# Thirteen more turns of activations by transposing DMA instead of TensorE

## The reference

```
def first_block(x, ...):
    proj = rmsnorm(x, norm1_w) @ w_in                    # feeds two branches, y_a and y_b
    mixed = gate_a * (y_a @ w_branch_a) + gate_b * (y_b @ w_branch_b)
    x = x + mixed @ w_out
    gu = rmsnorm(x, norm2_w) @ w_gate_up                 # 2048 -> 2 x 5632
    x = x + (silu(gu[:5632]) * gu[5632:]) @ w_down       # 5632 -> 2048
    return rmsnorm(x, norm_f_w)

def second_block(x, ...):
    proj = rms_norm(x, attn_norm_g) @ w_in               # feeds two token mixers
    h = x + concatenate([gla_out, nsa_out]) @ w_out
    m = rms_norm(h, ffn_norm_g)
    return h + (silu(m @ w_gate) * (m @ w_up)) @ w_down
```

## Time and profile before

| | us |
|---|---|
| median of 3 runs | 2662.98 |
| profiled execution, its own time | 2662.39 |
| its span, from first to last instruction | 2660.5 |
| TensorE busy in it | 2633.9 (99%) |
| ScalarE busy | 1329.6 (50%) |
| GpSimd busy | 1191.8 (45%) |
| VectorE busy | 1065.1 (40%) |

### The profile page before, as it was taken

How to read it: one execution, slowest core, us unless ns; L and a number is a source line. 1 busy time by engine, 2 the same in 40 slices (tenths; PEclk the granted TensorE clock), 3 DMA queues, 4 the chain that set the end, 5 groups by cost and what they waited for, 6 DMA issues and landing times. The chain is left out here.

```text
span 2660.5 us, 30430 instructions
## 1 busy us (share of the span) xinstructions
PE 2633.9 (99%) x12124; PEld 2172.7 (82%) x12124; DVE 1065.1 (40%) x1251; ACT 1329.6 (50%) x1654; POOL 1191.8 (45%) x535
## 2 busy tenths in 40 slices
PE   8999999999999999999999999999999999999999
PEld 6888787788888888888888878878888888888887
DVE  6577754433332222223332357446432322222222
ACT  6545445444445555555444465555455555554333
POOL 3576553344444444444444446333344444444443
PEclk9999999999999999999999999999999999999999
DMA  6444454365555666666555544454456666665554
GB/s 249 175 173 162 145 187 169 143 220 185 182 189 199 204 212 203 202 208 205 188 202 195 208 146 148 157 202 143 143 185 211 201 208 205 208 205 191 202 206 145
DMA packets 116844, 499.57 MB, mean 188 GB/s; under 512 B 50795, under 2 KB 53836, under 8 KB 59360
## 3 DMA queue, kind: packets, MB, share of 16 engines
q1 hardware_dynamic: 116704, 497.64, 54.5%
HBM read 485.02 MB, written 2.10 MB: 183 GB/s over the span
## 5 line engine op out<-in xcount | busy, mean ns | idle before, releaser
L2681 POOL TENSOR_TENSOR WL<-RAW,WH 128x1024 fp32r<-128x1024 f32 x441 | 1074.8, 2437 | 1423.0 <-ACT WH L1177 1422.8
L1177 ACT ACTIVATE WH<-RAW 128x1024 fp32r<-128x1024 f32 x889 | 939.6, 1058 | 1219.6 <-PE PB L633 1201.8
L1826 DVE TENSOR_TENSOR WL<-RAW,WH 128x1024 fp32r<-128x1024 f32 x448 | 603.8, 1348 | 1490.8 <-ACT WH L1177 1490.5
L629 PE MATMUL PB<-WH,HNH 128*128 128x512 f32 x2464 | 972.2, 395 | 5.1 <-ACT WH L1177 2.3
L633 PE MATMUL PB<-WL,HNH 128*128 128x512 f32 x2464 | 961.6, 390 | 6.7 <-DVE WL L1826 3.8
L630 PE MATMUL PB<-WH,HNL 128*128 128x512 f32 x2464 | 959.8, 390 | 0.0
L633 PEld LDWEIGHTS PB<-WL,HNH 128*128 128x128 f32 x2464 | 463.0, 188 | 107.4 <-DVE WL L1826 5.2
L629 PEld LDWEIGHTS PB<-WH,HNH 128*128 128x128 f32 x2464 | 463.3, 188 | 107.1 <-issue 11.7
L630 PEld LDWEIGHTS PB<-WH,HNL 128*128 128x128 f32 x2464 | 463.6, 188 | 94.0
L629 PE MATMUL PB<-WH,HDH 128*128 128x512 f32 x704 | 274.3, 390 | 0.0
L633 PE MATMUL PB<-WL,HDH 128*128 128x512 f32 x704 | 273.9, 389 | 0.0
(11 more groups left out here) (369 smaller groups left out, 1854.5 us busy)
## 6 DMA issues: line engine op xcount, KB each, us to landing
RAW<-in_w_gu SPq DMA_DIRECT2D x176, 1024.0 KB, 4.8
RAW<-in_w_dn SPq DMA_DIRECT2D x88, 1024.0 KB, 4.7
RAW<-in_w_in_a SPq DMA_DIRECT2D x55, 1024.0 KB, 4.8
RAW<-in_w_in SPq DMA_DIRECT2D x45, 1024.0 KB, 4.8
RAW<-in_w_out SPq DMA_DIRECT2D x32, 1024.0 KB, 4.7
RAW<-in_w_ga SPq DMA_DIRECT2D x24, 1024.0 KB, 4.7
RAW<-in_w_gb SPq DMA_DIRECT2D x24, 1024.0 KB, 4.8
WIN<-in_win SPq DMA_DIRECT2D x8, 512.0 KB, 5.7
```

What stands on the lines that cost most here:

```text
L629: e.matmul(o, hi[:, k, x], WH[:, s, c], start=k == 0, stop=False)
L1177: e.activation(WH[:, u % NSPL, :], RAW[:, n % NRAW, half * SU * 128:(half + 1) * SU * 128], ACT.Copy).then_inc(*wt.act.mark(("wh", u)))
L1826: e.tensor_tensor(WL[:, u % NSPL, :], RAW[:, n % NRAW, half * SU * 128:(half + 1) * SU * 128], f32(WH[:, u % NSPL, :]), ALU.subtract).then ...
L2681: e.tensor_tensor(WL[:, u % NSPL, :], RAW[:, n % NRAW, half * SU * 128:(half + 1) * SU * 128], f32(WH[:, u % NSPL, :]), ALU.subtract).then ...
```

## The change

Thirteen more turns of 512 columns go the way of the planes: MIX groups 0 to 2 (split in gb), X groups 0 to 2 for the first feed-forward (split in wo), X groups 0 to 2 for the second block (split in dn1), X groups 0 and 1 for the second feed-forward (split in mn), and the hidden group 10 of both feed-forwards. The last group of MIX and of X in each stage, and X group 2 in mn, are still turned by TensorE. The code that waits, splits, joins and rounds on ScalarE, with the tile numbers at which it stands:

```diff
@@ -1557,6 +1603,49 @@
                     e.activation(flat(MXH[:, k:k + 2, :]), bank("mx", g, q)[:, :], ACT.Copy).then_inc(
                         *m.act.mark(("mx", g, q)))
 
+            def split(planes, src, *name):
+
+                for h in range(2):
+                    if h == 0 and by_dma.index(name):
+                        e.wait_ge(*turn_before(*name))
+                    e.activation(planes[:, h, :, :], halves16(src[:, h, :]), ACT.Copy).then_inc(
+                        *m.act.mark(("planes", *name, h)))
+
+            def joined(dst, src, q, *name):
+
+                if q == 0:
+                    e.wait_ge(*turn_landed(*name))
+                e.activation(halves16(flat(dst)), two_tiles(src, q), ACT.Copy).then_inc(*m.act.mark(("joined", *name, q)))
+
+            def mix_split(g):
+                for h in range(2):
+                    e.wait_ge(*m.dve.done("mix", g, h))
+                split(XP, MIX[:, :, columns(g)], "mx", g)
+
+            def mix_joined(g, q):
+                k = 4 * g + 2 * q
+                joined(MXF[:, k:k + 2, :], MXP[:, g, :, :], q, "mx", g)
+
+            def mix_rounded(g):
+                e.wait_ge(*m.act.done("joined", "mx", g, 1))
+                k = slice(4 * g, 4 * g + 4)
+                e.activation(flat(MXH[:, k, :]), flat(MXF[:, k, :]), ACT.Copy).then_inc(
+                    *m.act.mark(("mx", g, 0), ("mx", g, 1)))
+
+            def x_split(planes, stage, step, g):
+                for h in range(2):
+                    e.wait_ge(*m.dve.done(*step, g, h))
+                split(planes, X[:, :, columns(g)], "hn", stage, g)
+
+            def x_joined(stage, g, q):
+                k = 4 * g + 2 * q
+                joined(HNF[:, k:k + 2, :], HNP[:, g, :, :], q, "hn", stage, g)
+
+            def x_normed(stage, gain, g):
+                e.wait_ge(*m.act.done("joined", "hn", stage, g, 1))
+                for k in range(4 * g, 4 * g + 4):
+                    normed(stage, k, gain, HNF[:, k, :])
+
             def normed_turned(stage, gain, g):
                 for q in range(2):
...
-                    e.wait_ge(*wt.pe.done("nt", NT["gb"] + 13))
-                after(64, 18, *([lambda: normed_turned(1, "norm2", g - 1),
-                                 lambda: token_squares(1, ("x", "wo"), g - 1)] if g else [lambda: mixed(3)]))
+                for k in tiles(64):
+                    if g == 0 and k == 18:
+                        mixed(3)
+                    if g and k == 8:
+                        x_split(XP, 1, ("x", "wo"), g - 1)
+                    if g and k == 18:
+                        token_squares(1, ("x", "wo"), g - 1)
+                    if g and k in (44, 48):
+                        x_joined(1, g - 1, (k - 44) // 4)
+                    if g and k == 54:
+                        x_normed(1, "norm2", g - 1)
 
             def ffn(stage, before, gain, gu, dn):
-                def planes(j, h):
-
...
-
-                def joined(j, q):
-
-                    if q == 0:
-                        e.wait_ge(*planes_landed(stage, j))
-                        if j == 0:
-                            e.wait_ge(*wt.pe.done("nt", NT[before] + 7))
+                def hidden_split(j):
+                    for h in range(2):
+                        e.wait_ge(*m.dve.done("z", stage, j, h))
+                    split(ZP, SIG, "z", stage, j)
+
+                def hidden_joined(j, q):
                     k = 4 * j + 2 * q
-                    e.activation(flat(ZF[:, k:k + 2, :]).bitcast(U16).rearrange("p (n s) -> p s n", s=2),
-                                 ZTP[:, j, :, :].rearrange("p (s k) n -> p s k n", s=2)[:, :, 2 * q:2 * q + 2, :].rearrange(
...
             w.rest()
             for g in range(4):
-                if g == 1:
-                    e.wait_ge(*wt.pe.done("nt", NT["nq1"] + 1))
-                after(32, 18, *([lambda: normed_turned(3, "ffn", g - 1),
-                                 lambda: token_squares(3, ("x", "mn"), g - 1)] if g else []))
+                for k in tiles(32):
+                    if g in (1, 2) and k == 9:
+                        x_split(XP, 3, ("x", "mn"), g - 1)
+                    if g and k == 16:
+                        token_squares(3, ("x", "mn"), g - 1)
+                    if g >= 2 and k in (16, 20):
+                        x_joined(3, g - 2, (k - 16) // 4)
+                    if g >= 2 and k == 24:
+                        x_normed(3, "ffn", g - 2)
+                    if g == 3 and k == 28:
```

SyncE issues the transposes, and TensorE's hooks go:

```diff
-                    e.wait_ge(*wt.pe.done("nt", NT[before] + 7))
+
+            def turned_by_dma(dst, planes, *name):
+
+                if by_dma.index(name):
+                    e.wait_ge(*turn_before(*name))
                 for h in range(2):
-                    e.wait_ge(*m.act.done("planes", stage, j, h))
...
+                                e.wait_ge(*wt.pe.done("nt", NT[before] + 7))
+                            turned_by_dma(ZTP[:, j - 1, :, :], ZP, "z", stage, j - 1)
+
+            def gains(g):
+                e.dma_start(GNF[:, g % 2, :], A["normf"][:, columns(g)]).then_inc(landed[f"gain{g % 2}"], 16)
+
+            for g in range(4):
+                for k in tiles(96):
+                    if g and k == 20:
+                        if g == 1:
+                            e.wait_ge(*wt.pe.done("nt", NT["ga"] + 15))
+                        turned_by_dma(MXP[:, g - 1, :, :], XP, "mx", g - 1)
+            for g in range(4):
+                for k in tiles(64):
+                    if g and k == 20:
...
+                        turned_by_dma(ZTP[:, 10, :, :], ZP, "z", 1, 10)
+                    if g == 0 and k == 60:
+                        e.wait_ge(*turn_landed("z", 1, 10))
+                        gains(0)
+                        gains(1)
+                    if g and k == 36:
...
+                    if g in (1, 2) and k == 20:
+                        if g == 1:
+                            e.wait_ge(*wt.pe.done("nt", NT["nq1"] + 1))
+                        turned_by_dma(HNP[:, g - 1, :, :], XP, "hn", 3, g - 1)
             gate_up(3, "mn")
             for g in range(4):
...
-                group(nt, HNH, HNL, 16, None, {16: lambda: turn_mix(g - 1)} if g else {})
+                group(nt, HNH, HNL, 16)
                 if g == 0:
...
-                      {16: lambda: turn_x(1, ("x", "wo"), g - 1) if g else turn_mix(3)})
+                      {} if g else {16: lambda: turn_mix(3)})
 
             def ffn(stage, before, gu, dn):
...
-                    elif stage == 1:
-                        hook = lambda: turn_x(2, ("xn",), g - 1)
-                    group(NT[dn] + 2 * g, HDH, HDL, 44, None if g else hidden_ready, {16: hook} if hook else {})
+                    group(NT[dn] + 2 * g, HDH, HDL, 44, None if g else hidden_ready)
 
             ffn(1, "wo", "gu1", "dn1")
...
                 group(NT["mn"] + 2 * g, MNH, MNL, 8, None if g else heads_ready,
-                      {16: lambda: turn_x(3, ("x", "mn"), g - 1)} if g else {})
+                      {16: lambda: turn_x(3, ("x", "mn"), 2)} if g == 3 else {})
```

In dn1, ScalarE splits at tile 24, SyncE issues at 36, ScalarE joins at 64 and 70 and rounds at 76; hidden group 10 is split at tile 6, issued at 28 and joined at 70 and 78. The split of hidden groups 0 to 9 is moved from tiles 6 and 14 to both at 6. VectorE's steps:

```diff
+            def mix_remainder(g):
+                k = slice(4 * g, 4 * g + 4)
+                e.wait_ge(*m.act.done("mx", g, 1))
+                e.tensor_tensor(flat(MXL[:, k, :]), flat(MXF[:, k, :]), f32(flat(MXH[:, k, :])), ALU.subtract).then_inc(
+                    *m.dve.mark(("mx", g, 0), ("mx", g, 1)))
+
+            def x_remainder(stage, gain, g):
+                for k in range(4 * g, 4 * g + 4):
+                    e.wait_ge(*m.act.done("hn", stage, k))
+                    e.scalar_tensor_tensor(out=HNL[:, k, :], in0=HNF[:, k, :], scalar=vec(gain, k), in1=f32(HNH[:, k, :]),
+                                           op0=ALU.mult, op1=ALU.subtract).then_inc(*m.dve.mark(("hn", stage, k)))
+
...
-                after(64, 22, (lambda: normed_turned(1, "norm2", g - 1)) if g else (lambda: mixed(3)))
+                for k in tiles(64):
...
+                        x_remainder(1, "norm2", g - 1)
                 e.wait_ge(landed[f"xx{g}"], 16)
                 residual("wo", g)
 
             def ffn(stage, gain, gu, dn):
-                def hidden(j):
-                    lows((HDL, HDH), ("z", stage), ("hd", stage), j)
-
                 def remainder(j):
                     k = 4 * j
...
-                after(32, 22, *([lambda: normed_turned(3, "ffn", g - 1)] if g else []))
+                for k in tiles(32):
+                    if g >= 2 and k == 28:
+                        x_remainder(3, "ffn", g - 2)
+                    if g == 3 and k == 30:
```

More of the change, by code:

```diff
@@ L156, in build @@
         IDENT = bump("IDENT", [128, 128])
+        TMP = at("TMP", [128, 2, 2, 512], U16, cur[0])
         TM = bump("TM", [128, 4, T])
@@ L195, in columns, with turn_landed, turn_before, halves16 @@
             return slice(512 * g, 512 * g + 512)
-        def planes_landed(stage, j):
-            return landed["planes"], 32 * (j + 1 + (10 if stage == 3 else 0))
```

(55 more changed lines are left out.)

78 lines of the change are left out of this document (44 added, 34 removed).

## The result

| | before | after |
|---|---|---|
| median of 4 runs each, us | 2663.34 | 2687.45 |
| lowest to highest | 2662.03 to 2663.86 | 2686.13 to 2688.77 |
| span of the profiled execution | 2660.5 | 2684.2 |
| ratio, 95% interval | | 1.0095 (1.0082 to 1.0107) |

The account below looks back on a forecast made before the run. TensorE, busy 99% of the span, was taken to bound the kernel. Turns -12.05, wo +21.6, gb +5.1 and mn +6.8 make +21.5 us: 2683.9, or 2684.5 on the median's scale; range 2666 to 2692.

Parts of the forecast that it names:

- Turns, -12.05: Thirteen turns leave TensorE: ten at 0.89 us and three in gb at 1.05, 12.05 us less.
- wo, 21.6 forecast: Three wo groups: TensorE waits 7.2 us each for the bank VectorE's residual frees, 21.6 us (12 to 25).
- The second case: VectorE's HNL gets in before GpSimd: wo costs 14.4 us, mn 5.6, total +13.1, 2676 us; chance 0.26.
- gb, 5.1 forecast: Three gb groups: TensorE waits 1.7 us each for the bank ScalarE's sigmoid frees, 5.1 us (3 to 8.4).
- The sign given for it: After gb's 64 tiles TensorE idles for a bank released by ScalarE's TM, 1.7 us, three times.
- mn, 6.8 forecast: mn groups 2 and 3: residuals come late, 4.2 and 2.6 us, together 6.8 (5.6 to 8).
- lower case of 3.0: mn group 2: residual 3.0 us late, against 5.4 if the fourth HNL meets GpSimd's low half.
- At nothing: dn1, hidden group 10 and moving the second split to tile 6 were taken to cost no waits.
- The fourth case: Loads come late behind the transposes; each of eleven pairs adds about 1 us: 2695 us; chance 0.06.
- The third: Joins don't hold ScalarE, or banks don't hold TensorE: 2657.7 or 2651 us; chance 0.11.
- the fifth: No measurable change: waits about half as large, 12 us, pay for the turns: 2663 us; chance 0.07.
- One sign that was given for the forecast: In the changed profile, TensorE's busy time falls by about 10 us or more.

Follow-up runs that it names:

- the run with earlier issue: Changed kernel with SyncE issuing gb's and wo's transposes at tile 16, ahead of tile 17's load, instead of tile 20: 2672.25 us, 1.0037 to the kernel before.
- five turns alone: Changed kernel with only dn1's three X groups and both hidden groups 10 by DMA; gb, wo, mn as before: 2657.48 us, 0.9984 to the kernel before.
- HNL behind the residual: Changed kernel with VectorE's four HNL in wo placed behind the two residuals instead of ahead: 2673.90 us, 1.0049 to the kernel before.

## Why the prediction was right, and where its sizes were off

The result is the forecast's: +24.1 us where +21.5 was worked out, and in wo, its largest term, by the chain that it named. That the sum is so near is in part luck: wo and mn came out 2.4 and 3.2 us dearer, gb 2.4 cheaper. Step by step:

**Turns, -12.05: right.** dn1's period fell to 59.84, gb's in the run with earlier issue to 32.64, and five turns alone gave 4.10 of 4.45. By the Trainium skill's figure ("TensorE: Matmul & The Clock Gate", "Part 4: PE-mode transpose", some 275 ns each), the 40 transposes of those five turns would be an estimated 11 us. The durations agree with it (270 to 331 ns), the time does not, as they overlap.

**wo, 21.6 forecast, 24.0 measured: the mechanism right, two sizes off against each other.** Issue at S + 11.25 (11.2 forecast); landing S + 18.6 (19.7), as the pair needed 7.4 us, just under the lower bound of 7.8; the join waited 3.7 (4.8); GpSimd went before HNL, as taken; the bank was free 30.4 us after S (31.7). So TensorE waited 5.7 a group, not 7.2: 17.2 in all. The 6.2 us of the slow clock were not in the sum at all: a wait was priced at its own length. They made good what the early landing took away; it is luck that the total is nearer than the steps. The second case fell by the order of the rows at 740.37 and 740.53. It would have been no cheaper: in the run with earlier issue VectorE began first and HNL still took 3.78.

The Trainium skill's "SBUF — State Buffer", "SBUF: two separate sides", calls the port pair an exclusive lock, held for a whole instruction. The trace agrees in that four HNL took 1.67 us alone and 3.75 and 3.78 beside one low half of GpSimd's (2.4 us). With earlier issue the first HNL took 0.48, GpSimd started beside it at 734.92, and the second HNL took 2.59, to 0.27 us past GpSimd's end. Each HNL is an instruction of its own, so that VectorE was first with the first of them did not help the second.

**gb, 5.1 forecast, 2.7 measured.** The landing was the cause, as forecast (the waits went when it came earlier), and the term was too large because it came 0.9 us earlier than taken, at S + 19.3. The sign given for it was wrong in part: TensorE was to wait 1.7 us for the bank, and it waited first for GpSimd's low half, a wait that the working of gb did not have, and then for the bank. That was free at about S + 25.2 and due at S + 24.5, so by this trace an estimated 0.7 us would have been lost there without the low half too.

**mn, 6.8 forecast, 10.0 measured.** Here a step was missed. ScalarE's second split, in group 2, needs the planes' buffer that the transposes of group 1 read. ScalarE and then SyncE in mn:

```profile
1937.03 2.00 ACT L1611 ACTIVATE XP<-X 128x1024 uint16<-128x1024 uint16 x2 [2.42 <-DMA HNP<-XP]
...
1941.12 2.57 ACT L1618 ACTIVATE HNF<-HNP 128x1024 uint16<-128x1024 uint16 x2
...
1929.56 5.32 SPq L544 DMA_TRANSPOSE HNP<-XP  x2
```

The transposes issued at 1929.56 had landed at 1937.0, 7.4 us later; a group of mn has 10.88 us, and the split stood at tile 9, so it waited 2.42. The prediction put the landing at 8.8 and the splits ahead of 7.2 in the same group. It reckoned with the landing only for the join (`turn_landed`), and not with the same count in `turn_before`, which the split waits for. In wo and gb a group is long enough to hide it. TensorE then waited 0.45 us at 1942.52 for GpSimd's low half, which hangs on the rounding behind that split. It waited 4.38 at 1948.08, where HNL met no low half of GpSimd's, and ran slowly for ten matmuls (2.2 us), and 2.14 at 1964.47, with no slow stretch behind it. By the distances between starts group 2 lost 5.2 us and 2.3 to the slow clock, group 3 lost 2.4; the forecast had 4.2, nothing and 2.6. Less the 2.4 of the split, group 2 comes to an estimated 2.8, near its lower case of 3.0.

**At nothing: right.** In dn1 ScalarE's joins waited 0.8 us in all for the planes, and no period there is longer than its units; hidden group 10 gave its 0.89 (with five turns only, the stretch from mn's first residual to dn2's, in which no other turn is gone, is 574.8 us against 575.7 before). The fourth case, late loads, did not come: no wait of TensorE's is put down to a load, and its waits for WL by GpSimd are seven of 1.4 us at most.

**The other cases.** The third (no join waits) and the fifth (waits of half the size) fell with the waits of 3.7 and 4.4 us at the joins. One sign that was given for the forecast was wrong: TensorE's busy time should have fallen by 10 us and rose by 0.4. Forty transposes fewer gave 4.1 less in the run where nothing waits; here the slow matmuls put it back.

## What to carry to other kernels

A DMA that replaces work of the bounding engine is free only if its landing fits between the step that fills its source and the step that reads its result. Read that landing at its place in the queue: here it was 7.4 us for a pair behind a load and 4.2 for one issued ahead of it. Find for every waiting instruction what is queued behind it, and for every buffer who must have read it before it is filled again. Put the instructions that free a bank ahead of those whose result is needed later: that order alone was worth 11.8 us here. Price a wait of TensorE's at more than its length, since the clock that comes after it may be lower.

## What the runs showed of the hardware beyond the forecast

- **The clock after a wait.** Behind waits of 5.8, 5.8, 5.6 and 4.4 us TensorE ran at the level of 1.2 GHz (granted clock 0.50 in 773 to 777 us) for 6 to 12 matmuls, 1.5 to 2.6 us lost each time. The three waits of 2.69 us with earlier issue had a slow stretch after the second only (granted clock 0.69 in 764 to 767, 1.00 in 739 to 742 and in 790 to 794). With HNL behind the residual the waits of 2.15 had one twice, and 0.73 had none; 2.14 us at 1964.47 in the changed kernel had none either. So around 2 to 3 us the length of the wait does not decide it alone; what does is open.
- **The time of a pair of transposes** depends on what is ahead of it. Behind a load issued 0.4 us before, the two held SyncE for 5.3 us and had landed after 7.4; issued ahead of that load, at 718.18, they held it for 2.60 and had landed after 4.2.
- **Port sharing where the order did not help.** Four short VectorE operations lost 2.1 us to one GpSimd operation of 2.4, whichever of the two engines started first.
